# Interleaving the high-weight and low-weight matmuls of the gate and up projections in a decoder trunk

## What is computed

```python
D_MODEL, SEQ, DEPTH, D_FF = 1024, 256, 2, 2816

def swiglu(h, w_gate, w_up, w_down):
    return (jax.nn.silu(h @ w_gate) * (h @ w_up)) @ w_down

for layer in range(DEPTH):
    x = x + 0.5 * swiglu(rmsnorm(x, norm_w[layer, 0]), ffn_w_gate[layer, 0], ffn_w_up[layer, 0], ffn_w_down[layer, 0])
    x = x + mixer(rmsnorm(x, norm_w[layer, 1]))
    x = x + cross_attention(rmsnorm(x, norm_w[layer, 2]), memn, xattn_wq[layer], xattn_wkv[layer], xattn_wo[layer])
    x = x + 0.5 * swiglu(rmsnorm(x, norm_w[layer, 3]), ffn_w_gate[layer, 1], ffn_w_up[layer, 1], ffn_w_down[layer, 1])
return rmsnorm(x, final_norm_w)
```

## Time and profile before

| | |
|---|---|
| median of 3 runs | 1231.47 us (1231.23 to 1231.47) |
| the profiled execution's own time | 1231.18 us |
| its span, first to last instruction | 1229.4 us |
| mean granted TensorE clock | 0.998 |
| TensorE busy | 1216.2 us (99%) |
| weight loads busy | 1080.5 us (88%) |
| VectorE busy | 777.3 us (63%) |
| ScalarE busy | 624.2 us (51%) |
| GpSimd busy | 89.8 us (7%) |

### The profile page before, as it was taken

The page is one execution under the profiler, slowest core; times in us unless marked ns, Lnnn a source line. Parts: engine busy times, 40 slices in busy tenths (PEclk is TensorE's granted clock), DMA queues, the critical chain, the costliest instruction groups (busy, mean ns, idle before and its releaser), DMA issues.

```text
span 1229.4 us, 18627 instructions
## 1 busy us (share of the span) xinstructions
PE 1216.2 (99%) x7511; PEld 1080.5 (88%) x7511; DVE 777.3 (63%) x824; ACT 624.2 (51%) x848; POOL 89.8 (7%) x98
## 2 busy tenths in 40 slices
PE   8999999999999999999999999999999999999997
PEld 7888889999989888888898888899978998888886
DVE  5766766864655576666676666665685656666664
ACT  5554546553454554444464444454566535545443
POOL 0000001640110020000020000020000101000002
PEclk9999999999999999999999999999999999999999
DMA  9866654454443466565555565645532433756550
GB/s 316 309 215 182 194 195 147 155 160 157 140 145 138 137 206 198 179 203 177 182 188 195 180 204 176 200 138 167 176 136 71 147 128 107 239 185 201 177 202 34
DMA packets 172548, 214.79 MB, mean 175 GB/s; under 512 B 14800, under 2 KB 155216, under 8 KB 172368
## 3 DMA queue, kind: packets, MB, share of 16 engines
q1 hardware_dynamic: 171920, 213.17, 52.9%
q0 software_dynamic: 144, 0.52, 0.1%
q10 hardware_dynamic: 432, 0.36, 0.1%
HBM read 213.00 MB, written 1.05 MB: 174 GB/s over the span
## 4 chain that ended last, share of the span: by engine, by line
PE 97%; DVE 1%; ACT 1%; DMA 1%; POOL 0%; issue 0%; SPq 0%; POOLq 0%; DVEq 0%; ACTq 0%
PE ps L1715 25%; PE ps L1694 16%; PE ps L1695 16%; PE ps L1696 16%; PE ps L1730 14%; PE ps L1955 1%; PE ps L1933 1%; PE ps L1770 1%; PE ps L2297 1%; PE ps L2169 1%; DVE w_lo L1064 1%; DMA xn<-in_xT 1%; PE ps L2319 0%; PE ps L2261 0%; PE ps L2258 0%; DVE hT L1087 0%
## 5 line engine op out<-in xcount | busy, mean ns | idle before, releaser
L1715 PE MATMUL ps<-hT,w_hi 128*128 128x512 f32 x1392 | 331.8, 390 | 2.3 <-issue 1.3
L1715 PEld LDWEIGHTS ps<-hT,w_hi 128*128 128x128 f32 x1392 | 257.9, 188 | 54.4 <-ACT w_hi L662 1.5
L1182 DVE TENSOR_TENSOR w_lo<-raw,w_hi 128x2048 fp32r<-128x2048 f32 x108 | 247.6, 2292 | 61.1 <-ACT w_hi L731 61.1
L1064 DVE TENSOR_TENSOR w_lo<-raw,w_hi 128x2048 fp32r<-128x2048 f32 x89 | 202.9, 2288 | 85.3 <-ACT w_hi L617 84.8
L617 ACT ACTIVATE w_hi<-raw 128x2048 fp32r<-128x2048 f32 x88 | 168.1, 1914 | 122.3 <-PE ps L1696 117.7
L731 ACT ACTIVATE w_hi<-raw 128x2048 fp32r<-128x2048 f32 x108 | 205.8, 1906 | 0.1
L1730 PEld LDWEIGHTS ps<-hT,w_lo 128*128 128x128 f32 x1408 | 180.4, 191 | 7.4 <-DVE w_lo L1064 0.7
L1730 PE MATMUL ps<-hT,w_lo 128*128 128x256 f32 x1408 | 182.7, 283 | 0.3 <-DVE w_lo L1064 0.3
L1694 PE MATMUL ps<-w_hi,arena_r 128*128 128x512 f32 x352 | 138.0, 392 | 0.0
L1695 PE MATMUL ps<-w_lo,arena_r 128*128 128x512 f32 x352 | 137.5, 391 | 0.0
L1696 PE MATMUL ps<-w_hi,arena_r 128*128 128x512 f32 x352 | 137.0, 389 | 0.0
(11 more groups left out here) (282 smaller groups left out, 1791.7 us busy)
## 6 DMA issues: line engine op xcount, KB each, us to landing
raw<-in_ffn_w_up SPq DMA_DIRECT2D x44, 1024.0 KB, 5.1
raw<-in_ffn_w_down SPq DMA_DIRECT2D x44, 1024.0 KB, 4.8
raw<-in_ffn_w_gate SPq DMA_DIRECT2D x43, 1024.0 KB, 5.1
raw<-in_xattn_wkv SPq DMA_DIRECT2D x16, 1024.0 KB, 5.5
raw<-in_even_w_in SPq DMA_DIRECT2D x13, 1024.0 KB, 5.1
raw<-in_xattn_wq SPq DMA_DIRECT2D x8, 1024.0 KB, 5.1
raw<-in_xattn_wo SPq DMA_DIRECT2D x8, 1024.0 KB, 4.8
raw<-in_odd_w_in SPq DMA_DIRECT2D x8, 1024.0 KB, 5.4
```

What stands on the lines that cost most here:

```text
L1064: ins = V.tensor_tensor(lo, src, hi.bitcast(F32), ALU.subtract)
L1182: V.tensor_tensor(w_lo[:, m % RING, :], raw[:, m % RING, :], w_hi[:, m % RING, :].bitcast(F32), ALU.subtract).then_inc(lo_done, 1)
L1715: mm(ps[:, bank0 + m, :], cols(w_hi, n, k, CW, m * P, (m + 1) * P), hT[:, k, :, :].rearrange("p a c -> p (a c)"), start=k == 0, stop=False)
```

## The change

`wide` replaces `wide_hi` and `wide_lo` in the 80 chunks of the 40 turns: for each pair (m, k) the high step and at once the low step of the same pair. Both waits, on `hi_done` and on `lo_done`, stand ahead of the chunk. `wide_staggered` serves six of the eight chunks ahead of the turns (the first of f = 1 and f = 2, the second of all four blocks): eight high steps of bank 0, the wait on `lo_done`, then eight high steps of bank 1 that alternate with the eight low steps of bank 0, and eight low steps of bank 1. The first chunk of f = 0 and of f = 3 stays as it was. The number of matmuls, their shapes and their operands stay the same.

```diff
+            def wide_high(n, bank, m, k):
+                mm(ps[:, bank, :], cols(w_hi, n, k, CW, m * P, (m + 1) * P),
+                   hT[:, k, :, :].rearrange("p a c -> p (a c)"), start=k == 0, stop=False)
+
+            def wide_low(n, bank, m, k):
+                return mm(ps[:, bank, SEQ:], cols(w_lo, n, k, CW, m * P, (m + 1) * P), hT[:, k, 0, :],
+                          start=False, stop=k == KT - 1)
+
+            def wide(n, bank0):
+
+                for m in range(2):
+                    for k in range(KT):
+                        wide_high(n, bank0 + m, m, k)
+                        last = wide_low(n, bank0 + m, m, k)
+                return last
+
+            def wide_staggered(n, bank0):
+
+                for k in range(KT):
+                    wide_high(n, bank0, 0, k)
+                pe.wait_ge(lo_done, n + 1)
+                for k in range(KT):
+                    wide_high(n, bank0 + 1, 1, k)
+                    wide_low(n, bank0, 0, k)
+                for k in range(KT):
+                    last = wide_low(n, bank0 + 1, 1, k)
+                return last
+
...
                 else:
                     pe.wait_ge(hT_done, 4 * w + 4)
                     pe.wait_ge(hi_done, base + 1)
-                    wide_hi(base, 0)
-                pe.wait_ge(lo_done, base + 1)
-                used(wide_lo(base, 0))
+                    used(wide_staggered(base, 0))
+                if f in (0, 3):
+                    pe.wait_ge(lo_done, base + 1)
+                    used(wide_lo(base, 0))
                 pe.wait_ge(hi_done, base + 2)
-                wide_hi(base + 1, 2)
-                pe.wait_ge(lo_done, base + 2)
-                used(wide_lo(base + 1, 2))
+                used(wide_staggered(base + 1, 2))
...
                     pe.wait_ge(hi_done, j * 3 + (n + 1 - 3))
-                    wide_hi(n, 0)
                     pe.wait_ge(lo_done, j * 3 + (n + 1 - 3))
-                    used(wide_lo(n, 0))
+                    used(wide(n, 0))
...
                     pe.wait_ge(hi_done, j * 3 + (n + 2 - 3))
-                    wide_hi(n + 1, 2)
                     pe.wait_ge(lo_done, j * 3 + (n + 2 - 3))
-                    used(wide_lo(n + 1, 2))
+                    used(wide(n + 1, 2))
```

## The result

The changed kernel takes 1239.18 us (1239.03 to 1239.37, 4 runs) against 1231.47 us: 7.7 us slower, a ratio of 1.0063 with a 95% interval of 1.005 to 1.0077. The forecast was 1230.5 us with a range up to 1236, so it missed.

The account below looks back on a forecast made before the run. TensorE's step-to-step pace was taken as the bound. Pairs +1.3 us and borders -2 us gave about -1 us on 1231.18, so 1230.2; the median's 0.3 above made it 1230.5 us, range 1222 to 1236.

Parts of the forecast that it names:

- What bounds the kernel: Whole span: TensorE is busy 99%, the clock is at 2.4 GHz, and only TensorE's pace from step to step counts.
- The one place that I had called tight: Second chunk of block 0: the wait on `lo_done` comes at 17.06, `w_lo` is ready at 16.83, 0.2 us to spare.
- The load doesn't limit the low steps: Low steps: a weight load can be had every 110 ns or so, a low step takes 120.
- The earlier wait: Wait on `lo_done` ahead of the chunk: costs nothing in steady turns, as the low part is ready 6 us earlier.
- the price of the pair: Alternating steps: low 114 instead of 120, high 234 instead of 227; 348 ns against 347, +1.3 us over 1328 pairs.
- rival 2: Alternating chunks: every high step costs what the worst does, low ones win nothing; slower, up to 1243 us; chance 0.19 or part.
- mild form: Alternating pairs: low 114 and high 236, 350 ns a pair, +4 us less 1 us at the borders, 1234.5 us.
- far end: Alternating pairs at worst: high 236 and low 120, 356 ns a pair, +12 us, 1243 us; chance about 0.08.
- three outcomes: Whole kernel: no measurable change 0.52, faster or part of it 0.29, slower or part of it 0.19.
- The borders: Gate-to-up and up-to-down borders, 40 each: recovery of 20 to 30 ns goes, fully or in part; -0.8 to -2.4, taken as -2 us.
- The signs: Changed profile: high starts 347 ns apart, gate and up chunks 5.55 us, turn 16.53 to 16.57; above 16.65 if slower.
- Rival 1: Alternating chunks: low steps keep 114 ns, high stay at 227; pair 341 ns, 1222 us; chance 0.29 or part.

## Why the prediction was wrong

**What bounds the kernel** was right: TensorE's pace alone, no wait, the same clock. No wait held up a step of the turns. The one place that I had called tight, the second chunk of block 0, had less to spare than the 0.2 us forecast: TensorE came 0.3 us earlier than before and lost 9 ns there.

**The load doesn't limit the low steps**: right as far as the runs go. Steps of 384 columns, with 50 ns more room for a load, lose at least as much; steps of 512 lose nothing.

**The earlier wait costs nothing**: right, 1231.20 us. **The staggered starts** cost nothing that can be measured: 1231.37 us.

**The step that failed is the price of the pair.** I took "each high step after one low step" as "the first of its kind in the trace, 234 instead of 227", and each low step behind a high one as 114, so 348 ns a pair. The first change in the changed kernel has just these values. The next ones don't: in the cycle of three pairs that repeats, high steps take 233, 241 and 236 ns and low ones 117, 120 and 113, 353 ns a pair in the mean. Both singles were read rightly from the earlier trace rows, but they held for a step with settled neighbours. The second high step, still at some 396 there, said that a change isn't over after one step; I gave that warning to rival 2, whose mild form (114 and 236, 350 ns, 1234.5 us) was the nearest case. The measured pair lies between it and its far end of 356 ns. Of the three outcomes I gave slower the smallest chance, 0.19, and cut the range at 1236, between those two ends.

**The borders** were booked with the wrong sign. I let -2 us come from the recovery that falls away. The down chunk has a slow start as before and takes 5.503 us in place of 5.468: 0.035 x 36 = +1.3 us. One low step ahead, in this rhythm, leaves more to settle than sixteen; behind the 347 ns rhythm the down chunk takes 5.467, as before. Of the 27 ns that the up chunk took beyond the gate chunk, 10 are left.

**The signs.** The changed profile was to have high steps 347 ns apart; by the sum's own 114 and 234 it should have said 348. The trace has 353. A turn above 16.65 us was the sign named for rival 2, and it came, at 16.79; the last sentence of the prediction, that it fails if single steps cost neither what the first after a switch nor what a settled one costs, came true with the 241.

With measured prices the sum closes. A turn grows from 16.574 to 16.793, its three chunks by 0.101 + 0.083 + 0.035 = 0.22 us; the 36 turns of the loops make 7.9 us. The four first turns take 0.11 off (0.05 us more in block 0, 0.05 less in each of the others), the staggered chunks add 0.23. That is 8.0 us; TensorE came to the second chunk of block 0 some 0.3 us earlier (14.95 against 15.24), and the spans differ by 1237.2 - 1229.4 = 7.8 us.

**Rival 1** (a pair of 341 ns) was never seen as a rhythm in the changed kernel; only the first pair of a gate chunk, behind the long steps of the down chunk, takes 340 (227 + 113). The Trainium skill (TensorE: Matmul & The Clock Gate, on the back-to-back issue gap) has N / 2.4 + 2.5 ns as the gap of an isolated warm matmul; the prediction left out that the page means an isolated one. In the changed kernel the mean low step stands at 281 - 163 = 118 ns, not at the page's 109. It gained 2 ns on the 120 of before, and the high steps lost 8 (398 against 390).

**What stays open** is what the state is. It is carried from one step to the next, it hangs on what stands ahead of a chunk and on timing by nanoseconds, and steps of equal length always settled at the same pace here (227 ns for 512 columns, 173 for 384, 120 for 256). What in the machine holds it, no run here tells; nor do they show a rule that says which entry gives which rhythm. None of the orders beat the kernel before. The 347 ns rhythm in all chunks would at best return what the borders cost, 0.04 us in each of 40 turns, an estimate of 1.6 us or 0.13%.

## What to carry to other kernels

On a TensorE-bound stretch keep matmuls of one length together: each border from short to long steps cost 20 ns for runs of four and more, and an alternation 0, 7 or 13 ns for each pair, by its entry and its lengths. A step's price read at one switch is not the price of a stream of switches; where a change makes a new pattern and TensorE is at 99%, allow 2 to 3% of the pair (here 7 of 347 and 13 of 400 ns) and measure the pattern by itself. If the same instructions show two paces in one trace, look at what stands ahead of each stretch, and compare other traces of the same code before calling that the cause.

## What the runs showed that I had not expected

- An alternation of 512 and 256 columns ran in two stable rhythms, 347 and 353 ns a pair, for up to 32 pairs each.
- An alternation of 512 and 384 columns ran in two as well, 406 to 407 and 413 ns a pair against 400 for settled steps, and the entry that gave the cheap rhythm with 256 columns gave the dear one here. With 512 and 512 nothing was lost.
- The same eight pairs behind the same code ran at 347 ns in five traces and at 353 in six.
- Runs of two cost 3 ns a border, runs of four 19 ns: 1231.90 against 1235.78 us.
